# Half of a decoder layer's final residual added by accumulating DMA instead of by VectorE and TensorE

## What is computed

```python
def rms_norm(x, g):
    xf = x.astype(jnp.float32)
    y = xf * lax.rsqrt(jnp.mean(xf * xf, axis=-1, keepdims=True) + EPS)
    return (y * g.astype(jnp.float32)).astype(x.dtype)

        x = x + rms_norm(y, g_mix_post[l])          # "x1" below

        h = rms_norm(x, g_ffn_pre[l])
        f = conv_glu_ffn(h, w_up[l], conv_w[l], conv_b[l], w_down[l])
        x = x + rms_norm(f, g_ffn_post[l])
```

## Time and profile before

| what | us |
|---|---|
| median of 3 runs | 2048.89 (2047.55 to 2049.93) |
| the profiled execution | 2046.55 |
| its span, first to last instruction | 2044.8 |

### The profile page before, as it was taken

The page is one execution under the profiler, slowest core; times in us unless marked ns, Lnnn a source line. Parts: engine busy times, 40 slices in busy tenths (PEclk is TensorE's granted clock), DMA queues, the critical chain, the costliest instruction groups (busy, mean ns, idle before and its releaser), DMA issues.

```text
span 2044.8 us, 31852 instructions
## 1 busy us (share of the span) xinstructions
PE 2002.3 (98%) x12526; PEld 1802.7 (88%) x12526; DVE 1506.7 (74%) x1934; ACT 1018.4 (50%) x1563; POOL 0.7 (0%) x6
## 2 busy tenths in 40 slices
PE   8999999999999889999999999999999999999997
PEld 6888888888887789999999999999999887888785
DVE  5522543444446789888989888988898998889888
ACT  7422433445435655555555555555555654555453
POOL 0000000000000000000000000000000000000000
PEclk9999999999999989999999999999999999999999
DMA  8433232221535623523442343235223896877684
GB/s 320 136 127 119 78 93 83 80 65 63 226 124 190 222 83 129 174 101 111 156 137 101 122 167 115 101 130 173 101 102 115 308 319 234 279 259 228 201 297 158
DMA packets 220306, 323.28 MB, mean 158 GB/s; under 512 B 10543, under 2 KB 142031, under 8 KB 217853
## 3 DMA queue, kind: packets, MB, share of 16 engines
q1 hardware_dynamic: 219484, 316.00, 45.7%
q10 hardware_dynamic: 672, 5.24, 0.6%
HBM read 281.06 MB, written 44.07 MB: 159 GB/s over the span
## 4 chain that ended last, share of the span: by engine, by line
PE 87%; DVE 7%; ACT 3%; issue 2%; DMA 1%; DVEq 0%; SPq 0%; ACTq 0%
PE ring L2099 12%; PE ring L2101 12%; PE ring L2100 11%; PE ring L2360 10%; PE ring L2361 9%; PE ring L2362 9%; PE side L2360 4%; PE side L2361 4%; PE side L2362 4%; PE side L2099 2%; PE side L2100 2%; PE side L2101 2%; PE side L2175 1%; PE side L2148 1%; DVE w_lo L1780 1%
## 5 line engine op out<-in xcount | busy, mean ns | idle before, releaser
L1780 DVE TENSOR_TENSOR w_lo<-q,w_hi 128x1024 fp32r<-128x1024 f32 (+1 forms) x262 | 308.0, 1176 | 88.2 <-ACT w_hi L1271 69.7
L1501 DVE TENSOR_TENSOR w_lo<-raw,w_hi 128x512 fp32r<-128x512 f32 x256 | 169.6, 688 | 275.1 <-ACT w_hi L1054 275.1
L2360 PE MATMUL ring<-s_hi,w_hi 128*128 128x256 f32 x1008 | 287.4, 285 | 7.6 <-ACT snaps L1363 4.3
L2361 PE MATMUL ring<-s_lo,w_hi 128*128 128x256 f32 x1008 | 286.9, 285 | 0.0
L2362 PE MATMUL ring<-s_hi,w_lo 128*128 128x256 f32 x1008 | 286.8, 285 | 0.0
L1780 DVE TENSOR_TENSOR w_lo<-raw,w_hi 128x1024 fp32r<-128x1024 f32 x214 | 249.1, 1171 | 45.0 <-ACT w_hi L1271 26.9
L1054 ACT ACTIVATE w_hi<-raw 128x512 fp32r<-128x512 f32 x256 | 151.6, 623 | 188.2 <-PE ring L2101 172.8
L1271 ACT ACTIVATE w_hi<-q 128x1024 fp32r<-128x1024 f32 x174 | 183.5, 1056 | 97.7 <-PE side L2362 54.2
L2360 PEld LDWEIGHTS ring<-s_hi,w_hi 128*128 128x128 f32 x1008 | 195.2, 194 | 8.1 <-ACT snaps L1363 4.7
L2360 PE MATMUL ring<-a_hi,w_hi 128*128 128x256 f32 x688 | 196.0, 285 | 3.2 <-issue 3.2
L2099 PE MATMUL ring<-w_hi,act_hi 128*128 128x512 f32 x488 | 192.9, 395 | 3.3 <-DVE w_lo L1501 2.7
(11 more groups left out here) (313 smaller groups left out, 4598.9 us busy)
## 6 DMA issues: line engine op xcount, KB each, us to landing
q<-in_w_up SPq DMA_DIRECT2D x65, 1024.0 KB, 4.9
raw<-in_w_in SPq DMA_DIRECT2D x28, 1024.0 KB, 5.4
raw<-in_w_out SPq DMA_DIRECT2D x24, 1024.0 KB, 5.0
raw<-in_w_up SPq DMA_DIRECT2D x23, 1024.0 KB, 6.3
q<-in_w_down SPq DMA_DIRECT2D x66, 256.0 KB, 4.1
raw<-in_w_down SPq DMA_DIRECT2D x66, 256.0 KB, 4.1
q<-in_w_down SPq DMA_DIRECT2D x22, 512.0 KB, 4.1
q<-sa_d SPq DMA_DIRECT2D x22, 512.0 KB, 5.7
```

Source lines behind the costliest of these rows:

```text
L1501: dve.tensor_tensor(w_lo[:, s, q], raw[:, s, q], w_hi[:, s, q].bitcast(F32), ALU.subtract).then_inc(lo_done, 1)
L1780: dve.tensor_tensor(lo, src, hi.bitcast(F32), ALU.subtract).then_inc(hp_lo_done, 1)
L2360: pe.matmul(dst, hi, b_hi, start=first, stop=False, skip_group_check=True)
L2361: pe.matmul(dst, hi, b_lo, start=False, stop=False, skip_group_check=True)
```

## The change

Half 0 of x1 is spilled straight into its place in the output, and half 1 to a smaller `x1_d`; each spill is now two transfers of 512 KB, and those who waited for 16 on `x1_out` wait for 32. Only half 1 is read back. At the end ScalarE scales half 0 of each tile by rstd in place (`row_scale`, 128x1024), and GpSimd issues four accumulating transfers that add those rows onto the output in HBM. TensorE's eight row products, ScalarE's two diagonals and four copies are gone, and VectorE finishes half 1 only. VectorE's order at the end changes too.

```diff
-        (x1_back_at,) = overlay(("x1_back_at", [P, TT, D], F32))
+        (x1_back_at,) = overlay(("x1_back_at", [P, TT, 2, BLK], F32))
...
             def spill_x1(t):
                 sp.wait_ge(x1_ready, 2 * t + 2)
-                sp.dma_start(x1_d[t], resid[:, t, :]).then_inc(x1_out[t], 16)
+                x = resid[:, t, :].rearrange("p (h n c) -> p h n c", h=2, n=2)
+                sp.dma_start(out_half(0, t), x[:, :, 0, :]).then_inc(x1_out[t], 16)
+                sp.dma_start(x1_d[t], x[:, :, 1, :]).then_inc(x1_out[t], 16)
...
-            for n, t in ((1, 0), (1, 1), (0, 0), (1, 2), (0, 1), (0, 2), (1, 3), (0, 3)):
-                if n or t > 1:
-                    sp.wait_ge(out_ready, t + 1 if t < 2 else 2 * t - n)
-                else:
-                    sp.wait_ge(row_kept, 2 * t + 2)
-                sp.dma_start(out_d[:, t, :].rearrange("p (h n c) -> p h n c", h=2, n=2)[:, :, n, :],
-                             f_row(n, t)).then_inc(out_done, 16)
-            sp.wait_ge(out_done, 16 * 2 * TT)
+            for t in range(TT):
+                sp.wait_ge(out_ready, t + 1)
+                sp.dma_start(out_half(1, t), f_row(1, t)).then_inc(out_done, 16)
+            sp.wait_ge(out_done, 16 * TT)
...
+            for t in range(TT):
+                pool.wait_ge(x1_out[t], 32)
+                pool.wait_ge(row_scaled, t + 1)
+                pool.dma_start(out_half(0, t), f_row(0, t), accum_op=ALU.add).then_inc(row_added, 16)
+            pool.wait_ge(row_added, 16 * TT)
...
+            def row_scale(t):
+
                 act.wait_ge(rstd_ready, NB_F + t + 1)
-                act.activation(diagonal(t), ident[:, :], ACT.Copy, scale=rstd[:, NB_F + t, 0:1]).then_inc(diag_ready, 1)
...
+                act.wait_ge(f_gained, TT)
+                act.activation(f_row(0, t), f_row(0, t), ACT.Copy, scale=rstd[:, NB_F + t, 0:1]).then_inc(row_scaled, 1)
```

More of the change, by code:

```diff
@@ L517, in build @@
         copies = nc.dram_tensor("copies", [A_HEADS + B_HEADS, P, RLEN], F32)
[L518 removed]
+        x1_d = nc.dram_tensor("x1_d", [TT, P, 2, BLK], F32)
         sa_d = nc.dram_tensor("sa_d", [N_PAIRS, P, SA_OPS, HALF_S], F32)
@@ L749, in f_row, with out_half @@
             return (f0, f1)[n][:, t, :, :]
[L751 to L755, removed]
+        def out_half(n, t):
+            return out_d[:, t, :].rearrange("p (h n c) -> p h n c", h=2, n=2)[:, :, n, :]
         def w_at(v):
@@ L871, in load_early @@
                              (1 - i // 2) * 2 * P + col + 2 * P]).then_inc(early_in[i], 16)
-            sp.wait_ge(x1_out[0], 16)
+            sp.wait_ge(x1_out[0], 32)
             sp.wait_ge(h_scaled, 1)
             load_early(2, "22", 0)
-            sp.wait_ge(x1_out[1], 16)
+            sp.wait_ge(x1_out[1], 32)
             sp.wait_ge(h_scaled, 2)
@@ L1010, in _ @@
                         for t in rows_back:
-                            sp.wait_ge(x1_out[t], 16)
-                            sp.dma_start(x1_back_at[:, t, :], x1_d[t]).then_inc(x1_back, 16)
+                            sp.wait_ge(x1_out[t], 32)
+                            sp.dma_start(x1_back_at[:, t, :, :], x1_d[t]).then_inc(x1_back, 16)
                 if w == b1 + 2 * 8 + 1:
@@ L1458, in row_root @@
                                scale=1.0 / D).then_inc(root_ready, 1)
-            def row_diagonal(t):
-                if t == 0:
-                    act.wait_ge(a_lo_done, len(ITEMS))
+            def row_scale(t):
                 act.wait_ge(rstd_ready, NB_F + t + 1)
-                act.activation(diagonal(t), ident[:, :], ACT.Copy, scale=rstd[:, NB_F + t, 0:1]).then_inc(diag_ready, 1)
[L1467 to L1471, removed]
+                act.wait_ge(f_gained, TT)
+                act.activation(f_row(0, t), f_row(0, t), ACT.Copy, scale=rstd[:, NB_F + t, 0:1]).then_inc(row_scaled, 1)
             f_square(1, 0)
             row_root(0)
+            row_scale(0)
             f_square(1, 1)
             row_root(1)
[L1477 to L1483, removed]
+            row_scale(1)
+            f_square(1, 2)
+            row_root(2)
+            f_square(1, 3)
+            row_root(3)
+            row_scale(2)
+            row_scale(3)
         @block.vector
@@ L1832, in sum_s2 @@
                 dve.wait_ge(sum_ready, 2 * batch + 1)
-                dve.wait_ge(x1_out[2], 16)
+                dve.wait_ge(x1_out[2], 32)
                 add(batch_of(by_token_tile(s2_val[:, :, :]), batch), batch_of(by_token_tile(s1_val[:, :, :]), batch),
@@ L1855, in sum_to_lo @@
                 if op == OP_S4:
-                    dve.wait_ge(x1_out[3], 16)
+                    dve.wait_ge(x1_out[3], 32)
                 left_to_lo(LEFT_COUNT[op] - (batch == 0), lo, src, hi)
@@ L2060, in after, with finish @@
                                       ALU.add).then_inc(mean_ready, 1)
[L2062 to L2070, removed]
+            def finish(t):
+                f = f_row(1, t)
+                dve.wait_ge(f_gained, TT + t + 1)
+                dve.scalar_tensor_tensor(out=f, in0=f, scalar=rstd[:, NB_F + t, 0:1], in1=x1_back_at[:, t, :, :],
+                                         op0=ALU.mult, op1=ALU.add).then_inc(out_ready, 1)
             for w in range(H_DOWN + N_DOWN - 8):
@@ L2084, in _ @@
                 times_gain(TT + m, 1, m)
[L2085 to L2092, removed]
+                if m == 0:
+                    one_rstd(NB_F)
+                    finish(0)
+            dve.wait_ge(down_ready, 3)
+            sum_f(1, "21", 0)
+            one_rstd(NB_F + 1)
+            finish(1)
+            dve.wait_ge(down_ready, 4)
+            sum_f(1, "21", 1)
+            times_gain(TT + 2, 1, 2)
+            one_rstd(NB_F + 2)
+            finish(2)
+            one_rstd(NB_F + 3)
+            times_gain(TT + 3, 1, 3)
+            finish(3)
         @block.tensor
@@ L2463, in _ @@
                     mm.then_inc(down_ready, 1)
[L2464 to L2474, removed]
-                              start=False, stop=True).then_inc(row_added, 1)
 def kernel(**inputs):
```

3 lines of the change are left out of this document (1 added, 2 removed).

## The result

The change makes the kernel slower by about a quarter of a per cent, which is clear of no change. Thirteen executions of each kernel gave a median of 2047.55 us before (2046.67 to 2049.93) and **2052.79 us** after (2052.06 to 2053.80): a ratio of 1.0024, with a 95% interval of 1.0017 to 1.0031. The profiled execution took 2052.89 us, its span 2051.1 (2044.8 before).

The account below looks back on a forecast made before the run. TensorE was busy for 98% of the span, the end set by bytes in flight as much as VectorE. Spill and read-back 0, VectorE 3.3 us earlier, accumulating transfers leaving 0.7: 2048.9 - 0.7 = 2048.2 us, range 2045.3 to 2055.0.

Parts of the forecast that it names:

- Rival 2: At the end, GpSimd's accumulating transfers go one at a time, 6.4 us each: 4.9 us later, 2053.8 us; chance 0.22.
- What is late next: The step on the accumulating transfers at the end: 7.7 us of motion from 2035.5, span 2044.1, 0.7 us earlier.
- only the passes add up: At the end, bytes of other transfers cover one transfer's waits, so an accumulating one counts 2.56 us of motion.
- the two passes: In the final accumulating transfers, the destination is read, then written: 2.56 us of motion each, against 1.28 plain.
- the two earlier accumulating ones are through by then: Accumulating transfers ready at 2024.7 and 2030.1 were taken as done, leaving two accumulating and two plain from 2035.5.
- Tile 1's row: In the tail, ScalarE's new scale of tile 1 starts at 2029.08 and takes 1.04 us; row ready at 2030.1.
- VectorE's tail: At the end, two of six finishing operations go and the order changes: last finish at 2036.43, 3.3 us earlier.
- rival 1: At the end, adding costs the engines nothing, one pass each: span 2041.5, 3.3 us earlier, 2045.6 us; chance 0.17.
- Rival 3: At the end, VectorE's two-input operations keep GpSimd from preparing transfers until 2036.4: 3.1 us later, 2052.0 us; chance 0.08.
- the spill: Near 656 to 700 us, four 1 MB transfers become eight of 0.5 MB: 0, or 1.0 us if a load slips.
- the read-back: Near 1970 us, four transfers of 1 MB become four of 0.5 MB while TensorE is busy throughout: gain 0.
- TensorE's row products and their copies: At the end, eight row products, two diagonals and four PSUM copies were off the chain; removing them gives 0.

Follow-up runs that it names:

- e9: The kernel after with 1152 bytes a partition (72 places) for GpSimd's descriptors instead of 1024 (64 places); 2050.15 us, ratio 1.0018 to before.
- e1: The kernel after with 1536 bytes a partition (96 places) for GpSimd's descriptors instead of 1024; 2050.27 us, ratio 1.0017 to before.
- e3: The kernel after with plain GpSimd transfers in place of adding ones, so the output lacks half 0's residual; 2044.59 us, ratio 0.9986.
- e10: The kernel after with 1728 bytes a partition (108 places) for GpSimd's descriptors instead of 1024; 2051.62 us, ratio 1.0023 to before.
- e7: The kernel before with each spill in two transfers of 512 KB and the waits on it raised from 16 to 32; 2047.25 us, ratio 1.0000.
- e4: The kernel before with VectorE's new order alone, tile 1 finished ahead of the sum of tile 3's last quarter; 2047.65 us, ratio 1.0003.
- e6: The kernel after with 1088 bytes a partition (68 places) for GpSimd's descriptors instead of 1024; 2052.79 us, ratio 1.0028 to before.
- e8: The kernel before with adding by DMA for tile 0 only, tile 1 still over TensorE, and VectorE's new order; 2045.11 us, ratio 0.9992.
- e2: The kernel after with each adding transfer of 512 KB cut in two of 256 KB; 2055.19 us, ratio 1.0039.
- e5: The kernel after with adding by DMA for tiles 0 and 1 only, VectorE finishing both halves of tiles 2 and 3; 2045.97 us, ratio 0.9994.

## Why the prediction was wrong

The forecast was 2048.2 us, 0.7 earlier than before, with the adding transfers side by side. The kernel came out 5.2 us later. **Rival 2** (one at a time, 2053.8) was the case that came true in its form.

**The step that failed** is the one in "What is late next" by which the waits of one transfer are covered by the bytes of another and "only the passes add up". The forecast took from the sync queue that transfers of one queue overlap. On GpSimd's they need room in a store, and this kernel's holds one adding transfer: tile 1's was issued at 2032.93, tile 2's at 2039.12, tile 3's at 2045.21, and from 2044 to 2046 the engines stood all but idle (0.07).

**The sum, term by term.** The span was forecast at 2044.1 and came at 2051.1, 7.0 us later. Of that, 1.75 us had come by the start of tile 1's scale (2030.83 for 2029.08), and 5.25 came behind it (20.3 us for 15.0). Of the 5.25, 2.6 go with the store: they are gone in e9 and e1. The other 2.6 stay in e9, where from 2032 to 2045 us no microsecond has the DMA engines under a share of 0.93, and tile 2's wait for room, from 2034.4 to 2037.80, lies inside that stretch: there the engines' own time sets the end, and the term that was too small is the two passes. An adding transfer took 3.3 to 3.6 us of the engines instead of 2.56 (the packet times of GpSimd's queue in after and e9, over 16 engines), and three of them had to pass behind 2032, not two: that "the two earlier accumulating ones are through by then" failed too.

**Rival 2's own sum** was 2030.1 + 3 x 6.4 = 2049.3. Measured: 2032.93 + 6.19 + 6.09 + 5.4 = 2050.6, and the span ends 0.5 later. The periods were shorter than 6.4, the last (5.4) also than the 6.1 us from which it was said to decide; the start was 2.8 us later. That its 2053.8 lies within 1.0 us of the measured 2052.79 is in part luck: these two errors work against each other, and it was counted from a median that was 1.3 us too high. Its cause was put as a queue that doesn't start one transfer until the one before has left; the runs with 72 and 108 places show that this holds only where the store has no room, and e3 that it holds for plain transfers too.

**Tile 1's row** was due at 2030.1 and ready at 2030.83 + 1.15 = 2031.98. Of these 1.9 us, 0.1 is the scale, which took 1.15 instead of 1.04. The rest is TensorE's slow stretch, for which the sum had no term. Count from a matmul ahead of it that had waited some 1.95 us for VectorE in every kernel (at 2013.70 in before, at 2013.58 in after): the forecast has tile 1's scale 15.4 us behind it, and so have e9, e1 and e10, whose clock was at 1.00 there; the kernel after has 17.25. So the forecast for VectorE's new order was right to 0.1 us. From ready to issue took 0.95 us, of which 0.55 is there in e9 and e1 as well, where nothing waits; the rest is the wait for tile 0's landing (2026.38 + 6.3 = 2032.7).

**The passes.** Two passes, 2.56 us, was the forecast; an adding transfer with the engines to itself took 3.3, against 1.28 for a plain one (by the 409 GB/s of the earlier trace rows). That is 2.6 times, not 2. The Trainium skill, "Collectives: The Full Stack", section "The bandwidth ceiling: the fold count and why AG ≠ RS ≠ AR", gives the adding step of a collective half the rate of a copy, which is twice the time; carried over to this transfer it is too little, and the measurement decides. It weighs where the store doesn't: in e9 the last two go together, and the engines are full while little is moved, as this stretch of e9 shows.

```profile
2042.00:2044.00 2.00, 0.00 (x0) 0.00 (x0) 0.00 (x0) 0.00 (x0) 0.00 (x0) 0.50 1.12 185
```

So of the 7.0 us between e3 and the kernel after, from tile 1's scale to the end, 2.6 go with the store and 4.4 with the adding itself, most of it the engines' own time.

**VectorE's tail**: 3.3 us earlier was forecast, 1.4 came, for the late start above. In e3, with the whole of the relief and plain transfers, it is worth 2.4 us in time (2044.59 against 2046.94), with the slow stretch and the store's wait of 3.32 us still in it. So with free adding rival 1's 3.3 us may have been near; no run shows it.

**Rival 3** did not happen: tile 1's transfer was issued at 2032.93, between two finishing operations of VectorE (2030.83 and 2034.38), not after the last at 2038.3. In e9 and e10 tile 1's went 0.55 us after its row was ready, while VectorE ran the sum that starts at 2030.62. The Trainium skill, "SBUF — State Buffer", section "Who interferes with whom", says that tensor_tensor has no two-port mode, and infers that it leaves GpSimd the writing of descriptors. The trace agrees.

**Right** were the spill (0: e7) and the read-back (landings of 6.1 us, with TensorE busy for 4.00 of 4.00 us from 1978 as in the earlier trace rows). That TensorE's row products and their copies were worth nothing is not shown: they are in no link of the chain, but e4 shows the sync queue held by the last copy, and so was that of before, issued at 2037.38 behind a copy that ended at 2037.35. No run takes them away alone.

**The level.** I added to the shown median of three runs, 2048.89; the median of before in thirteen is 2047.55. The difference of the two kernels doesn't depend on it. The lower end of the range, 2045.3, is called rival 1's, whose own sum is 2045.6; nothing hangs on it.

## What stays open

TensorE's slow stretch near 2016 to 2022 us. After and e3 have one of 6.8 us, e6 and e8 one of 3.4; before, e1, e2, e4, e5, e7, e10 and e9 have none. The same columns, of e9:

```profile
2016.00:2022.00 6.00, 4.34 (x19) 3.61 (x20) 4.38 (x7) 2.05 (x5) 0.00 (x0) 1.00 0.01 3
```

e9 differs from the kernel after in 128 bytes of the store alone, so neither the adding nor VectorE's order nor the spill brings the stretch by itself. What the engine did ahead was alike too: 3.31 us busy of the six from 2010 in before, 3.53 in after (the last of them already at the lower clock). The four kernels that have the stretch here have less time at 1.2 GHz in the middle of the program, 10.2 us between 696 and 747 instead of 17.1; but e5 has the 10.2 and no stretch here. So its place moves between kernels that are nearly the same. Counted from the matmul near 2013.6 to VectorE's finish of tile 1, it costs 1.4 us in e6 and e8 and 1.9 in after and e3; in the middle the 6.8 us less bring after to that matmul only 0.1 us ahead of before. What decides the place wasn't found.

## What to carry to other kernels

A transfer issued by GpSimd is priced in two ways that a transfer of the sync queue here wasn't: by the places that it takes in the descriptor store (by the rule above two for each packet and engine, 34 for 512 KB added, 18 for the plain ones), and, if it adds, by some 2.6 times the engines' time. Before such transfers are put at the end of a kernel, count how many the store holds, and let none be the last: there each costs its full landing time, about 6 us here. A small dose early in the tail (e8, one tile) keeps the relief without the wait; that it beats the kernel before is likely, not shown.

## What was new about the hardware

- GpSimd's queue stalls on a store of descriptors: one by one at 64 and 68 places, at 72 and 96 the third alone with the fourth right behind it, and at 108 the fourth alone (7.87 us). Raising it from 64 to 72 brought 2.6 us of the tail; splitting the transfers made the time 2.4 us worse.
- A wait for room lasts until everything ahead has landed, not until enough has (e2's seventh piece, e10's fourth transfer).
- An adding transfer of 512 KB takes 3.3 to 3.6 us of the 16 DMA engines, a plain one 1.28.
- From a row's being ready to the start of GpSimd's instruction takes 0.55 to 0.62 us; the instruction itself 1.08 to 1.24 us for an adding transfer that goes alone, 0.68 to 0.80 for a plain one of the same bytes.
- A plain transfer of 512 KB from GpSimd is in no way slow: e3's landed in 3.0 to 4.1 us, as those of the sync queue do (3.0 to 4.6).
